# A decoder block on one core: one projection moved ahead of the S5 output, a quarter of the scan's carries moved to GpSimd, and GpSimd's low parts cut in four

## What is computed

```python
h = rmsnorm(x, norm_g)
proj = h @ w_in        # -> q | kc, vc | ksl, vsl | kwi, vwi | gl | gate_nsa | u | gate_s5 | mg
# NSA attention: three softmaxes for each head
#   compressed keys and values: gelu(blocks @ w1) @ w2 of kc and vc, 32 blocks of 16 tokens apart
#   selected (rotated ksl, vsl): top 16 of 8 blocks, so all causal keys;  window 512 (rotated kwi, vwi)
o_nsa = g0 * o_cmp + g1 * o_sel + g2 * o_win
branch_a = (o_nsa * silu(gate_nsa)) @ w_proj_nsa
# S5: x[t] = a * x[t-1] + Bbar u[t] (complex, 32 groups x 64 states);  y = Re(C x) + d * u
z = gelu(y);  o_s5 = z * sigmoid(z @ w_glu + b_glu)
branch_b = (o_s5 * silu(gate_s5)) @ w_proj_s5
out = rmsnorm(x + (sigmoid(mg_a) * branch_a + sigmoid(mg_b) * branch_b) @ w_out, final_g)
```

## Time and profile before

| | us |
|---|---|
| median of 3 runs (456.79 to 458.34) | 457.24 |
| the profiled execution, whole | 458.15 |
| its span (first to last instruction) | 456.4 |
| PE busy | 427.5 (94%) |
| DVE busy | 286.9 (63%) |
| ACT busy | 200.9 (44%) |
| POOL busy | 153.3 (34%) |

### The profile page before, as it was taken

How to read it: one execution, slowest core, us unless ns; L and a number is a source line. 1 busy time by engine, 2 the same in 40 slices (tenths; PEclk the granted TensorE clock), 3 DMA queues, 4 the chain that set the end, 5 groups by cost and what they waited for, 6 DMA issues and landing times.

```text
span 456.4 us, 7185 instructions
## 1 busy us (share of the span) xinstructions
PE 427.5 (94%) x2736; PEld 341.8 (75%) x2736; DVE 286.9 (63%) x653; ACT 200.9 (44%) x392; POOL 153.3 (34%) x78
## 2 busy tenths in 40 slices
PE   5899999999998599889998999999999999999993
PEld 5688888888777576546665677888888888888993
DVE  3668679799989959968999783153062070070545
ACT  6641777724234157885546541222222222241433
POOL 0332442433322101323131334444544444444430
PEclk9989999999999799989999999999999999999999
DMA  8944995124841254100101103654333333323104
GB/s 285 269 95 117 159 237 173 38 73 122 247 93 46 48 94 140 46 1 7 41 2 47 47 2 93 241 158 108 92 93 92 92 93 95 118 90 113 47 3 182
DMA packets 71266, 47.27 MB, mean 104 GB/s; under 512 B 20176, under 2 KB 66720, under 8 KB 71200
## 3 DMA queue, kind: packets, MB, share of 16 engines
q1 hardware_dynamic: 71072, 46.74, 38.4%
q10 hardware_dynamic: 160, 0.07, 0.1%
HBM read 42.61 MB, written 4.19 MB: 103 GB/s over the span
## 4 chain that ended last, share of the span: by engine, by line
PE 81%; DVE 8%; ACT 5%; issue 4%; DMA 1%; POOL 1%; POOLq 1%; ACTq 0%; DVEq 0%
PE bank L923 22%; PE bank L925 21%; PE bank L924 21%; PE bank L1231 3%; PE bank L1210 2%; PE bank L1192 2%; DVE prob L1668 2%; PE bank L1090 2%; DVE prob L1688 1%; PE bank L968 1%; PE bank L1223 1%; ACT z L871 1%; ACT prob L865 1%; PE bank L1036 1%; DMA hid<-in_norm_g 1%
## 5 line engine op out<-in xcount | busy, mean ns | idle before, releaser
L644 POOL TENSOR_TENSOR w_lo<-raw,w_hi 128x1024 fp32r<-128x1024 f32 (+3 forms) x56 | 133.6, 2386 | 241.1 <-ACT w_hi L673 241.1
L923 PE MATMUL bank<-hT_lo,w_hi 128*128 128x512 f32 x288 | 116.3, 404 | 2.7 <-DVE hT_lo L1369 1.8
L925 PE MATMUL bank<-hT_hi,w_hi 128*128 128x512 f32 x288 | 113.3, 393 | 0.0
L924 PE MATMUL bank<-hT_hi,w_lo 128*128 128x512 f32 x288 | 113.0, 392 | 0.0
L673 ACT ACTIVATE w_hi<-raw 128x1024 fp32r<-128x1024 f32 (+2 forms) x56 | 58.4, 1043 | 73.2 <-PE bank L925 73.1
L923 PEld LDWEIGHTS bank<-hT_lo,w_hi 128*128 128x128 f32 x288 | 54.5, 189 | 16.6 <-issue 5.8
L925 PEld LDWEIGHTS bank<-hT_hi,w_hi 128*128 128x128 f32 x288 | 54.5, 189 | 11.8
L924 PEld LDWEIGHTS bank<-hT_hi,w_lo 128*128 128x128 f32 x288 | 54.7, 190 | 10.5
L865 ACT ACTIVATE prob<-prob,nmax 128x128 f32<-128x128 f32 (+2 forms) x64 | 35.3, 553 | 22.0 <-DVE nmax L1668 21.9
L887 ACT ACTIVATE tmp<-bank 128x512 f32<-128x512 f32 x16 | 9.6, 597 | 59.9 <-PE bank L925 57.5
L1730 DVE SCALAR_TENSOR_TENSOR tmp<-tmp,bank 128x512 f32<-128x512 f32 x8 | 5.5, 687 | 44.6 <-ACT tmp L887 44.6
(11 more groups left out here) (228 smaller groups left out, 740.2 us busy)
## 6 DMA issues: line engine op xcount, KB each, us to landing
raw<-in_w_in SPq DMA_DIRECT2D x28, 512.0 KB, 3.9
raw<-in_w_in SPq DMA_DIRECT2D x16, 256.0 KB, 3.7
raw<-in_w_out SPq DMA_DIRECT2D x8, 512.0 KB, 3.7
x_sb<-in_x SPq DMA_DIRECT2D x4, 512.0 KB, 5.0
raw<-in_w_proj_s SPq DMA_DIRECT2D x4, 512.0 KB, 3.4
raw<-in_w_proj_nsa SPq DMA_DIRECT2D x8, 256.0 KB, 4.1
r_sb<-in_x SPq DMA_DIRECT2D x1, 2048.0 KB, 8.6
out<-r_sb SPq DMA_DIRECT2D x8, 256.0 KB, 2.2
```

The source lines that it names most:

```text
L644: nc.gpsimd.tensor_tensor(lo, whole, hi.bitcast(F32), ALU.subtract).then_inc(lo_done, 1)
L923: nc.tensor.matmul(dst, w[0], x[1], start=first, stop=False, skip_group_check=True)
L924: nc.tensor.matmul(dst, w[1], x[0], start=False, stop=False, skip_group_check=True)
L925: return nc.tensor.matmul(dst, w[0], x[0], start=False, stop=last, skip_group_check=True)
```

## The change

- TensorE: gn0's projection stands ahead of the S5 output (bank 4 now, Y in banks 0, 5, 6, 7); the PET transposes are moved into step 2 of the attention (banks 4, 5); the 7 parameter transposes are put in twos between the slices of u0, and the 32 of B in fours between the slices of u1; gn1's pieces are in steps 0 to 3.
- VectorE: `carry_in` for 12 of 16 group pairs; the compressed softmax's first half ahead of the gates and the copies of the compressed values; `powers` of pq and ps ahead of the rotations, `build_e(False, 0)` ahead of `rotate_q(2)`, and `build_e(True, 1)` from the middle of the scan to ahead of it.
- GpSimd: the last four group pairs' carries (eight operations of 448 elements, temporaries in SBUF), after gs3's low part and ahead of gn0's; every low part of a block, from u1 up to mgb0, in four instructions of a quarter each.
- ScalarE: `cmp_exp(0)`, gn0's tanh with the next split, `cmp_exp(1)`, then the eight copies of Y; the PET copies in step 2.

```diff
-FILL = dict(gn1=(1, 4), gn2=(7, 10), ...
+FILL = dict(gn1=(0, 3), gn2=(7, 10), ...
...
+    use("gn0", 4)
     for m in range(8):
-        use(f"Y{m}", (4, 0, 5, 6, 7)[m % 5])
-    use("gn0", 7)
-    for g, b in enumerate((3, 2)):
+        use(f"Y{m}", (0, 5, 6, 7)[m % 4])
+    for g, b in enumerate((4, 5)):
         use(f"PET{g}", b)
...
+            def carry_last_groups():
+                qs = slice(3 * GP // 4, GP)
+                shape = (P, GP // 4, RUN - 1, NRUN)
+                n = shape[1] * shape[2] * shape[3]
+                ta, tb = (t[:, 0:n].rearrange("p (q j m) -> p q j m", q=shape[1], j=shape[2])
+                          for t in (pb_sb, k_swap[:, 0, :]))
...
+                pl.wait_ge(starts_set, 1)
+                for ri, (s0, s1), op in ((0, (starts[0], starts[1]), ALU.subtract), (1, (starts[1], starts[0]), ALU.add)):
+                    nc.gpsimd.tensor_tensor(ta, s0, re, ALU.mult).then_inc(pool_carry, 1)
+                    nc.gpsimd.tensor_tensor(tb, s1, im, ALU.mult).then_inc(pool_carry, 1)
+                    pl.wait_ge(pool_carry, 4 * ri + 2)
+                    nc.gpsimd.tensor_tensor(inner[ri], inner[ri], ta, ALU.add).then_inc(pool_carry, 1)
+                    pl.wait_ge(pool_carry, 4 * ri + 3)
+                    nc.gpsimd.tensor_tensor(inner[ri], inner[ri], tb, op).then_inc(pool_carry, 1)
+                    pl.wait_ge(pool_carry, 4 * ri + 4)
...
-                nc.gpsimd.tensor_tensor(lo, whole, hi.bitcast(F32), ALU.subtract).then_inc(lo_done, 1)
+                parts = 1 if j == 0 or j >= split_at["mgb1"] else 4
+                size = lo.shape[1] * lo.shape[2] // parts
+                hi, lo, whole = (v.rearrange("p k n -> p (k n)") for v in (hi, lo, whole))
+                for c in range(0, parts * size, size):
+                    ins = nc.gpsimd.tensor_tensor(lo[:, c:c + size], whole[:, c:c + size], hi[:, c:c + size].bitcast(F32), ALU.subtract)
+                ins.then_inc(lo_done, 1)
...
+                if name == "gs3":
+                    carry_last_groups()
...
-            for m in range(4):
-                copy_y(m)
-            cmp_exp(0)
-            for m in range(4, 8):
-                copy_y(m)
-            cmp_exp(1)
-            for g in range(GROUPS):
-                evacuate(f"PET{g}", peT[:, g].rearrange("p i q -> p (i q)"), bk(f"PET{g}")[:, :])
...
             ac.wait_ge(bias_done, 1)
+            for m in range(2):
+                wait_fill(ac, f"SCC{m}")
+            cmp_exp(0)
             fill_part("gn0")
+            cmp_exp(1)
+            for m in range(8):
+                copy_y(m)
             for s in range(NS + LAG + 1):
                 w = s - LAG
+                if s == LAG - 1:
+                    for g in range(GROUPS):
+                        evacuate(f"PET{g}", peT[:, g].rearrange("p i q -> p (i q)"), bk(f"PET{g}")[:, :])
...
+            def parameter_columns(kt):
+                if kt == 2:
+                    pe.wait_ge(rows_in, 16 * 6)
+                    pe.wait_ge(dt_spread, 1)
+                    open_bank(pe, "PAR")
+                if 2 <= kt < 6:
+                    for n in range(2 * kt - 4, min(2 * kt - 2, 7)):
...
+            def b_columns(kt):
+                if kt == 0:
+                    pe.wait_ge(b_in, 16 * 2)
+                    open_bank(pe, "B")
+                for k in range(4 * kt, 4 * kt + 4):
...
+            channel_major("u0", "u0", wait_hT=True, between=parameter_columns)
+            channel_major("u1", "u1", between=b_columns)
             channel_major("u2", "u2")
...
             channel_major("gs3", "gs3", kts=(4, KT))
+            channel_major("gn0", "gn0")
             wait_drained(pe, "TT0")
             wait_drained(pe, "TT1")
             pe.wait_ge(scan_done, 1)
+            pe.wait_ge(pool_carry, 8)
             pe.wait_ge(e_built, 4)
...
-            channel_major("gn0", "gn0")
-            pe.wait_ge(cm_done, 1)
...
                 if s < NS:
                     scores(s)
+                if s == LAG - 1:
+                    turned_compressed()
...
+            powers(pq_sb, pw_sb[:, 0, CH - 1], pw_sb[:, 1, CH - 1], RUN)
+            powers(ps_sb, pq_sb[:, 0, RUN - 1], pq_sb[:, 1, RUN - 1], RUN2)
+            V.tensor_scalar(half_bias[:, :], bias_glu[:, :], 0.5, None, MUL).then_inc(bias_done, 1)
             ve.wait_ge(sin_set, 1)
             rotate_q(0)
             rotate_q(1)
-            powers(pq_sb, pw_sb[:, 0, CH - 1], pw_sb[:, 1, CH - 1], RUN)
+            build_e(False, 0)
             rotate_q(2)
-            powers(ps_sb, pq_sb[:, 0, RUN - 1], pq_sb[:, 1, RUN - 1], RUN2)
-            V.tensor_scalar(half_bias[:, :], bias_glu[:, :], 0.5, None, MUL).then_inc(bias_done, 1)
-            build_e(False, 0)
             rotate_q(3)
             build_e(False, 1)
             build_e(True, 0)
             rotate_k(0, sin_ps[:, :])
+            build_e(True, 1)
...
             flatten(1)
-            build_e(True, 1)
...
-            for q0 in (0, 4, 8, 12):
+            for q0 in (0, 4, 8):
...
-                         shape, scan_done if q0 == 12 else None)
+                         shape, scan_done if q0 == 8 else None)
```

## The result

The changed kernel took 451.28 us (median of 4 runs, 449.71 to 451.34) against 457.56 (4 runs, 456.79 to 458.34) for the kernel before beside it: a ratio of 0.9857, interval 0.9835 to 0.9878, so **6.3 us faster** where 9.4 were forecast. 451.28 lies inside the range and 3.5 above the predicted 447.8. The profiled execution took 451.25 with a span of 449.5.

A forecast was written before the change was run, and what follows sets the result against it. TensorE's 7.2 us idle at the scan's end, waiting on VectorE's carries, and half clock behind it were the loss. Terms -9.7 + 0.4 - 1.4 + 1.3 = -9.4 took the span from 456.4 to 447.0, median 447.8 us; range 443.8 to 452.0.

The forecast's parts named there:

- gn0 ahead, three groups: At the scan's end: gn0 before the S5 output and three VectorE carry groups start first scores 10.25 us earlier, net gain 9.7.
- VectorE's work after the scan: Behind the scan: VectorE's 13.4 us end at 161.7, before PET at 163.4, so cost zero with 1.7 us of cover.
- GpSimd's carries: Behind gs3's low part: eight operations of 1.12 us on GpSimd end at 142.2, cost zero.
- The rivals of 2.1 and 4.3 us an operation: GpSimd carries slow on broadcast operands, TensorE waits ahead of gn0: 456.2 us (10%, mostly partial) or about 473 (3%).
- Transposes between products: In u0 and u1: ten more changeovers at 0.3 us cost 3.0, less 1.65 of half clock saved, net cost 1.3.
- The credit of 1.65 for the stretch near 24 us: Early transposes: products on both sides keep the clock up, saving half of 3.3 us at half clock.
- changing over costs little: Rival for u0 and u1: the 3.0 us changeover cost vanishes and the clock stays up, 444.8 us; 15%.
- the clock falls for the length of u0 and u1: Rival: some 32 of 48 products run at half clock, 5.5 us plus the 1.65 not saved, 454.9 us; 7%.
- Low parts in four: Near 236 us: shorter GpSimd instructions hold VectorE's SBUF operation at most 0.7 us in place of 2.2, gain 1.4.
- the pieces win nothing: Rival: GpSimd's next piece takes the ports before VectorE, the 2.85 us stay, 1.4 us more, 449.2; 10%.
- The D term: Behind the S5 output's memory transfer: comes up at 172.8, y at 173.8, VectorE stands about 1.0 us, cost 0.4.
- offset of the profiled execution from its median: In the sum: the profiled 458.15 us was 0.9 above the median 457.24, so 448.75 was lowered to 447.8.

The follow-up runs named there:

- the second profile: The changed kernel, unaltered, timed and profiled again in a later group of runs: 449.71 us, 0.9846 of the kernel before.
- only the carries: Against the changed kernel: gn0 behind Y, parameter transposes in one piece, low parts whole, GpSimd's eight carries kept; 449.44 us, 0.9838 of the kernel before.

## Why the prediction was right, and 3.5 us off

**gn0 ahead, three groups: right in sum, the two moves not told apart.** From gs3's last product to the first scores the forecast was 10.25 us less; it was 21.76 - 11.40 = 10.36. The stall of 7.18 and the half clock behind it went as worked out. But the prediction took the two moves as one term and did not say which earns it. The runs separate them, from S to W: 27.87 us before; 23.84 with gn0 ahead alone (carry on VectorE); 18.45 with the carries alone; 17.51 with both. The first move is worth 4.0 and the second 9.4 by themselves, and together 10.4: they are two cures for one stall. Each of the three figures holds the 0.96 of the PET transposes, which only moved to behind W. That VectorE's work after the scan costs nothing was right for the changed kernel, where no wait came of it; with the full scan that work is what stops TensorE for 3.72 us inside Y.

**GpSimd's carries: right.** 1.12 us an operation forecast, 0.99 to 1.17 measured; end at 142.2 forecast, 144.7 measured in an execution that was 3.08 late by then. No wait of TensorE's came of it. The rivals of 2.1 and 4.3 us an operation fall.
The Trainium skill (GPSIMD Engine Reference, "Reconciling with measured numbers") gave an estimated 10.3 us for the group; from 135.84 to 144.72 it took 8.9, nearer to what the rows gave.

**Transposes between products: right in price; the credit beside it depends on luck.** 0.3 us a group and ten groups, 3.0, were charged; 3.11 came. The credit of 1.65 for the stretch near 24 us was taken too; in the second profile the early part is 1.45 longer, as forecast (1.3). In the first another stretch, at 17.4, cost 1.63. It had begun before the first interleaved transpose (18.76), so these didn't cause it. The rival "changing over costs little" falls, and so does "the clock falls for the length of u0 and u1". What the part was good for isn't shown: with the transposes in one piece three of five profiles (the kernel before is one) had a low clock between 24 and 38 us, and of the eight with the transposes spread, in twelve groups or three, none had one there. That points to a use, but in single executions; and where the stretch did come in one piece it cost 1.65, less than the 3.11.

**Low parts in four: the step that failed.** The gain of 1.4 rested on a hold of "at most 0.7 in place of 2.2" (which makes 1.5). The hold did become 0.7 (the operation of 2.85 took 1.22), but TensorE's waits went from 2.25 to 2.04: 0.2 us. The instructions behind the four pieces, `oT_lo` and `f_lo`, were whole, and VectorE, its own operation over sooner, met them with its normalisations, 0.34 us each, stretched to 1.37 and 1.28. The term is mis-sized: 0.2 where 1.4 was taken. The rival "the pieces win nothing" comes near in size and has its reason wrong: GpSimd's next piece did not go first, and the 2.85 us did not stay. VectorE and GpSimd took turns, one instruction each.
The Trainium skill (SBUF - State Buffer, "SBUF: two separate sides") has the ports locked for a whole instruction; the 1.37 and 1.28, which end with GpSimd's instructions, agree. That the two engines alternate is from the rows.

**The D term: no wait.** 0.4 was charged for a D term 9.7 us earlier. It came up 4.1 us earlier (177.65 for 181.76), 4.9 later than the 172.8 worked out, and yT was there 1.3 us ahead of it. Of the 4.9 the early part has 3.1. Most of the rest is a wait of VectorE's for TensorE, which the prediction did not have:

```profile
170.78 0.69 DVE L1720 COPY probT<-bank 128x512 f32<-128x512 f32 x1 [1.66 <-PE bank L1250]
```

With a piece of gn1 in step 0 and PET in step 2, TensorE reaches the first transposes of the attention 9.41 us behind W (170.08), where it took 7.26 before (175.21). The charge of 0.4 was avoided by this delay, not by a faster transfer.

**The clock behind the GELU.** Not in the prediction. Before, the products at 198.3 ran at half clock; after, they didn't. The post-GELU products came 5.15 us earlier and those at 203.40 before 6.69 (196.71). It gave back what the chain through the D term had lost: P is 6.52 earlier, the end 6.9. A wait of 2.20 us stands ahead of these products in both:

```profile
197.32 0.52 PE L1210 MATMUL bank<-ident,prob 128*128 128x128 f32 x3 [2.20 <-ACT probT L683]
...
198.79 0.63 PE L924 MATMUL bank<-hT_hi,w_lo 128*128 128x512 f32 x1
```
```profile
192.17 0.52 PE L1250 MATMUL bank<-ident,prob 128*128 128x128 f32 x3 [2.20 <-ACT probT L711]
...
193.45 0.39 PE L952 MATMUL bank<-hT_hi,w_lo 128*128 128x512 f32 x1
```

That the change is what keeps the clock up here is not shown. Of the eleven further profiles seven have a half-clock stretch somewhere from 180 to 194 us. These 1.5 us are luck as far as the runs tell.

**Where the 3.5 us are.** The span was to be 447.0 and was 449.5: 1.6 for the stretch at 17.4, 1.2 for the pieces, 0.4 to the good for the D term, the rest 0.1. Two terms that the prediction did not have cancel in this: between P and the post-GELU products the gain shrinks by 1.37 (6.52 to 5.15), and the clock behind the GELU gives 1.54 back. The last 0.9 are the offset of the profiled execution from its median, which I took off the new time as well. The 1.65 of the stretch near 24 us were already credited in full from that same execution, and such stretches are what makes an execution longer or shorter than the median: of nine further ones of the kernel before, that with a mean clock of 0.978 took 459.01 us and that with 0.989 took 455.49. The new kernel's profiled execution has no such offset (451.25 against 451.28). One effect was, it seems, counted twice; that is an argument from these times, and no run tests it. Against the 449.71 of the second group of runs the forecast is 1.9 off.

What stays open: why a half-clock stretch comes in one execution and not in the next of the same kernel, and whether the whole change has fewer of them than "only the carries". The mean clocks hint at it (0.998, 0.998, 0.997 and 0.991 against 0.997 and four of 0.988 to 0.993, on one chip), in too few executions to show it.

## What to carry to other kernels

When two moves cure one stall, undo each by itself before keeping both: here one of them alone gave as much as all four parts. Small operations of another shape between long products cost a changeover for each group here, however small the group was, so few and large groups were cheaper. Don't correct a forecast by the profiled execution's offset where a stretch that makes this offset is also a term of the sum.

## What was not expected of the hardware

- **One half-clock stretch more or less in the same program.** The changed kernel had S at 143.16 and at 141.53 us, with a granted clock of 0.51 and 1.00 from 17.4 to 20.8, and its times stand at 449.6 to 449.9 and at 451.25 to 451.34. Such stretches also came near 34, near 185 and near 236 us in some of the other profiles. A difference of 1.5 us between two single executions of this kernel says nothing.
- **Turns between VectorE and GpSimd.** With short instructions queued on both engines, each of the VectorE operations shown above waited for one GpSimd instruction and not for two: 0.34 us became 0.74 beside pieces of 0.7 and 1.28 to 1.37 beside instructions of 1.3. Cutting one instruction moved the wait to the next uncut one.
- **Changing between 128-row products and 16-row transposes** took 0.30 us for going over and back; a slice with four transposes behind it took 1.43 us in place of 0.69, of which the four are 0.44. On TensorE's timeline of the changed kernel, with the product before and the one behind:

```profile
25.05 0.39 PE L953 MATMUL bank<-hT_hi,w_hi 128*128 128x512 f32 x1
25.37 0.61 PE L1027 MATMUL bank<-ident,b_rows 16*128 16x16 f32 x4
25.91 0.50 PE L951 MATMUL bank<-hT_lo,w_hi 128*128 128x512 f32 x1
26.25 0.39 PE L952 MATMUL bank<-hT_hi,w_lo 128*128 128x512 f32 x1
```
